# A causal 31-tap convolution on four engines: eight taps moved to TensorE by shifted copies, VectorE's chunks staggered, six z blocks last

## What is computed

```python
def _odd_mixer(h, w_in, conv_w, conv_b, ln_g, ln_b, w_out):
    proj = h @ w_in                                # 1024 -> 3 * 1024
    val, gt, z = proj[:, :1024], proj[:, 1024:2048], proj[:, 2048:]
    g = val * sigmoid(gt)
    c = depthwise_causal_conv(g, conv_w)           # 31 taps, per channel
    c = c + conv_b
    cc = c - mean(c, channels)
    var = mean(cc * cc, channels)
    c = cc * rsqrt(var + LN_EPS) * ln_g + ln_b
    y = silu(c) * silu(z)
    return y @ w_out                               # then residual, final norm
```

## Time and profile before

| | us |
|---|---|
| median of three runs | 2760.51 (2759.78 to 2760.76) |
| the profiled execution | 2754.84 |
| its span | 2753.1 |
| mean granted TensorE clock | 0.948 |

### The profile page before, as it was taken

How to read it: one execution, slowest core, us unless ns; L and a number is a source line. 1 busy time by engine, 2 the same in 40 slices (tenths; PEclk the granted TensorE clock), 3 DMA queues, 4 the chain that set the end, 5 groups by cost and what they waited for, 6 DMA issues and landing times. The chain is left out here.

```text
span 2753.1 us, 31632 instructions
## 1 busy us (share of the span) xinstructions
PE 2559.3 (93%) x11316; PEld 2065.6 (75%) x11316; DVE 989.8 (36%) x1557; ACT 992.3 (36%) x1337; POOL 1294.9 (47%) x683
## 2 busy tenths in 40 slices
PE   8999999999999999999998889999999986978777
PEld 6888878656888888888885777788888875766556
DVE  3223130164522213322113612543223169214973
ACT  5333323376433333333332323343333332224442
POOL 5555544301555544555542433246555453346843
PEclk9999999899999999999998999889999988988998
DMA  3324323201232332232331221023233322321211
GB/s 137 96 94 134 111 92 107 77 1 32 76 99 92 99 107 77 99 97 94 101 106 54 71 83 61 1 77 100 94 96 99 107 80 66 83 76 62 64 58 62
DMA packets 69332, 228.34 MB, mean 83 GB/s; under 512 B 8804, under 2 KB 13284, under 8 KB 69133
## 3 DMA queue, kind: packets, MB, share of 16 engines
q1 hardware_dynamic: 63456, 218.63, 24.9%
q10 hardware_dynamic: 4956, 5.61, 0.8%
q0 software_dynamic: 848, 3.15, 0.3%
HBM read 222.75 MB, written 6.84 MB: 83 GB/s over the span
## 5 line engine op out<-in xcount | busy, mean ns | idle before, releaser
L366 POOL TENSOR_TENSOR wl_sb<-raw_sb,wh_sb 128x1024 fp32r<-128x1024 f32 x401 | 973.2, 2430 | 1055.5 <-ACT wh_sb L358 1052.1
L1651 PE MATMUL banks<-xh_sb,wh_sb 128*128 128x512 f32 x2064 | 815.7, 395 | 72.8 <-POOL wl_sb L366 56.2
L1652 PE MATMUL banks<-xh_sb,wl_sb 128*128 128x512 f32 x2064 | 810.6, 393 | 0.0
L1653 PE MATMUL banks<-xl_sb,wh_sb 128*128 128x512 f32 x2064 | 810.2, 393 | 0.0
L358 ACT ACTIVATE wh_sb<-raw_sb 128x1024 fp32r<-128x1024 f32 x401 | 423.8, 1059 | 809.7 <-DMA raw_sb<-weights 805.5
L1651 PEld LDWEIGHTS banks<-xh_sb,wh_sb 128*128 128x128 f32 x2064 | 392.4, 190 | 163.8 <-issue 53.7
L1652 PEld LDWEIGHTS banks<-xh_sb,wl_sb 128*128 128x128 f32 x2064 | 392.9, 190 | 81.5
L1653 PEld LDWEIGHTS banks<-xl_sb,wh_sb 128*128 128x128 f32 x2064 | 391.9, 190 | 82.4
L1651 PE MATMUL banks<-hh_sb,wh_sb 128*128 128x512 f32 x704 | 273.9, 389 | 0.0
L1652 PE MATMUL banks<-hh_sb,wl_sb 128*128 128x512 f32 x704 | 273.9, 389 | 0.0
L1653 PE MATMUL banks<-hl_sb,wh_sb 128*128 128x512 f32 x704 | 273.9, 389 | 0.0
(11 more groups left out here) (359 smaller groups left out, 2689.9 us busy)
## 6 DMA issues: line engine op xcount, KB each, us to landing
raw_sb<-weights SPq DMA_DIRECT2D x404, 512.0 KB, 3.5
scratch<-scratch ACTq DMA_DIRECT2D x1, 2560.0 KB, 12.2
x_sb<-x_in SPq DMA_DIRECT2D x8, 256.0 KB, 9.2
mix_sb<-scratch POOLq DMA_DIRECT2D x1, 2048.0 KB, 8.9
out<-hf_sb SPq DMA_DIRECT2D x8, 256.0 KB, 2.1
turn<-mix_sb SPq DMA_DIRECT2D x4, 256.0 KB, 4.6
mix_sb<-turn SPq DMA_DIRECT2D x4, 256.0 KB, 4.3
turn<-mix_sb ACTq DMA_DIRECT2D x4, 256.0 KB, 2.5
```

The lines of the kernel that those rows point to most:

```text
L366: pool.tensor_tensor(wl[:, slot, :], raw[:, slot, :], wh_f[:, slot, :], ALU.subtract).then_inc(w_split, 1)
L1651: pe.matmul(dst, wh[:, q, cols], in_hi, start=first, stop=False)
L1652: pe.matmul(dst, wl[:, q, cols], in_hi, start=False, stop=False)
L1653: return pe.matmul(dst, wh[:, q, cols], in_lo, start=False, stop=last)
```

## The change

- **Taps.** TensorE gets taps 0 to 7, VectorE taps 8 to 26 (19), ScalarE with GpSimd taps 27 to 30 (4).
- **TensorE's taps.** For each chunk SP issues 16 copies inside SBUF (`shifted`): for each partition quarter q (32 channels) and each shift j = 0 to 3, 32 rows of 516 columns go to partitions 32j to 32j+31 of `moved`. A matmul then contracts over 128 partitions, which are 4 taps x 32 channels, against a 128x32 matrix of tap weights (`tap_mat`, built by GpSimd, 128x512 for two chunks), and writes 32 output partitions with a tile position of its own. Eight matmuls of 512 columns a chunk (4 quarters, 2 groups of taps), all plain float32, go to bank 6 or 7 (`conv_taps`). TensorE issues them three blocks after the chunk's g block.
- ScalarE copies that bank out and adds the bias (`keep_pe_sum`), GpSimd adds it to the other taps' sum (`add_pe_sum`), both four blocks after the g block.
- **Order of GpSimd and ScalarE.** The additions of a chunk no longer stand together behind its gate product, but one and two blocks later; products and sums have two sets of buffers.
- **Order of VectorE.** A round takes the second ten steps of chunk c-1 alternating with the first ten of chunk c, so that chunk c starts as soon as its own gate product is there; nine rounds in all, the first and the last with one chunk alone.
- **Order of blocks.** `vgvgvgvgzvgvgzvgvgzzzzzz`: two z blocks stand among the v and g blocks, six stand last. All loops over the 24 blocks are written out.
- **Order on SP.** The 16 copies of a chunk wait for its gate product and stand between the weight loads: after the load of block b for which block b-4 was a g block.

```diff
-POOL_TAPS = 7
+TAPS_PE, TAPS_DVE, TAPS_POOL = 8, 19, 4
+ROWS_TAP = 32
+for _kind in "vgvgvgvgzvgvgzvgvgzzzzzz":
+    ODD.append((_kind, _of[_kind]))
+GATE_AT = {c: b for b, (kind, c) in enumerate(ODD) if kind == "g"}
...
+        def shifted(sp, c):
+            sp.wait_ge(g_mul, c + 1)
+            if c >= 2:
+                sp.wait_ge(pe_taps, c - 1)
+            for j in range(4):
+                for q in range(4):
+                    rows, dst = slice(ROWS_TAP * q, ROWS_TAP * (q + 1)), slice(ROWS_TAP * j, ROWS_TAP * (j + 1))
+                    sp.dma_start(moved[c % 2][dst, q, :], gpad[rows, c, j:j + LONG]).then_inc(g_moved[c % 2], 16)
+
+        def odd_in_tensor(pe, first_three):
+            def conv_taps(c):
+                pe.wait_ge(g_moved[c % 2], 256 * (c // 2 + 1))
+                pe.wait_ge(tap_weights, c // 2 + 1)
+                if c >= 2:
+                    pe.wait_ge(pe_kept, c - 1)
+                for a in range(TAPS_PE // 4):
+                    for q in range(4):
+                        last = pe.matmul(banks[ROWS_TAP * q:ROWS_TAP * (q + 1), 6 + c % 2, :],
+                                         tap_mat[c // 2 % 2][:, 8 * (c % 2) + 2 * q + a, :],
+                                         moved[c % 2][:, q, 4 * a:4 * a + T], start=(a == 0), stop=(a == 1),
+                                         tile_position=(0, ROWS_TAP * q))
+                last.then_inc(pe_taps, 1)
+
+            first_three("odd.in", "odd")
+            for b in range(3, len(ODD)):
+                pe.wait_ge(w_split, BLK["odd.in"] + b + 1)
+                if b >= 4:
+                    pe.wait_ge(tiles_freed, FREE0 + TILE["odd.in"] + b - 3)
+                block_mm(pe, lin[b % 4], b % 4, xh, xl)
+                for c in range(KD):
+                    if b == GATE_AT[c] + 3:
+                        conv_taps(c)
...
+            for b, (kind, c) in enumerate(ODD):
+                if b:
+                    high_part(act, "odd.in", b % 4, b - b % 4)
+                for other in range(KD):
+                    if b == GATE_AT[other] + 1:
+                        tap_products(other)
+                    if b == GATE_AT[other] + 4:
+                        keep_pe_sum(other)
+                act.wait_ge(blocks_done, BLK["odd.in"] + b + 1)
...
+            for c in range(KD + 1):
+                for n in range(half):
+                    if c > 0:
+                        tap_step(c - 1, half + n)
+                    if c < KD:
+                        tap_step(c, n)
...
-            loads(first + 12, BLOCKS)
+            loads(first + 12, BLK["odd.in"])
+            for b in range(len(ODD)):
+                some([BLK["odd.in"] + b])
+                if b >= 4 and ODD[b - 4][0] == "g":
+                    shifted(sp, ODD[b - 4][1])
+            loads(BLK["odd.out"], BLOCKS)
...
+            for b, (kind, c) in enumerate(ODD):
+                if b:
+                    low_part(pool, "odd.in", b % 4, b - b % 4)
+                if kind == "v" and c % 2 == 0:
+                    weights_of_taps(c // 2)
+                for other in range(KD):
+                    if b == GATE_AT[other] + 1:
+                        add_tap(other, 1)
+                        add_tap(other, 2)
+                    if b == GATE_AT[other] + 2:
+                        add_tap(other, 3)
+                    if b == GATE_AT[other] + 4:
+                        add_pe_sum(other)
+                if kind == "g":
+                    gated(b, c)
```

More of the change, by code:

```diff
@@ L89 @@
                   ("ssm_d", 4), ("conv_b", 8), ("ln_g", 8), ("ln_b", 8), ("head_g", 8), ("conv_w", 31 * 8),
-                  ("mconv_w", 4 * 16), ("log_dt", 16), ("a_re", 16), ("a_im", 16), ("b_i", 1), ("b_f", 1)):
+                  ("tap_w", 64), ("mconv_w", 4 * 16), ("log_dt", 16), ("a_re", 16), ("a_im", 16), ("b_i", 1), ("b_f", 1)):
     VEC[_name] = _c
@@ L98 @@
 C_ID, C_TRI, C_ONE, C_INV = 0, P, 2 * P, 3 * P
-NCONST = C_INV + 64
+C_STACK = C_INV + 64
+NCONST = C_STACK + ROWS_TAP
+ODD, _of = [], {"v": 0, "g": 0, "z": 0}
+for _kind in "vgvgvgvgzvgvgzvgvgzzzzzz":
+    ODD.append((_kind, _of[_kind]))
+    _of[_kind] += 1
+GATE_AT = {c: b for b, (kind, c) in enumerate(ODD) if kind == "g"}
 def skewed(scratch):
@@ L238, in build @@
         tap_prod = sem("tap_prod")
-        tap_sum = sem("tap_sum")
+        tap_sum = [sem(f"tap_sum{i}") for i in range(2)]
+        o_tap = [sem(f"o_tap{i}") for i in range(2)]
+        g_moved = [sem(f"g_moved{i}") for i in range(2)]
+        tap_weights = sem("tap_weights")
+        pe_taps = sem("pe_taps")
+        pe_kept = sem("pe_kept")
         std_ready = sem("std_ready")
@@ L459, in credits_vector @@
             dve.memset(unused(), 0.0).then_inc(conv_act, 2)
-            dve.memset(unused(), 0.0).then_inc(tap_sum, 1)
         def halve_vector(dve):
@@ L1481, in build @@
         tap_acc = sig_o
-        taps = [region(17408 + T * j, T) for j in range(POOL_TAPS)]
+        taps = [[region(17408 + T * (TAPS_POOL * q + j), T) for j in range(TAPS_POOL)] for q in range(2)]
+        pe_sum = [rstd[:, :], acc[:, :]]
+        LONG = T + 4
+        moved = [buf.rearrange("p (q n) -> p q n", n=LONG) for buf in (region(21504, 4 * LONG), hf_f[:, 0:4 * LONG])]
+        tap_mat = [hf_f[:, 4 * LONG + 512 * q:4 * LONG + 512 * (q + 1)].rearrange("p (s n) -> p s n", n=ROWS_TAP)
+                   for q in range(2)]
@@ new lines, in conv_weight, with conv_bank @@
+        def conv_weight(c, tap):
+            col = VEC["conv_w"] + CONV_K * c + tap
+            return vec[:, col:col + 1]
+        def conv_bank(c):
+            return banks[:, 4 + c % 2, :]
+        def shifted(sp, c):
[6 more added lines that the diff above has]
+                    sp.dma_start(moved[c % 2][dst, q, :], gpad[rows, c, j:j + LONG]).then_inc(g_moved[c % 2], 16)
@@ L1484, in odd_tensor @@
         def odd_tensor(pe):
             for c in range(KD):
-                pe.wait_ge(o_conv, c + 3)
+                pe.wait_ge(o_conv, c + 1)
                 last = pe.matmul(banks[:, 6, :], ones, cc[:, c, :], start=(c == 0), stop=(c == KD - 1))
@@ L1493, in odd_scalar @@
             act.wait_ge(o_v, 1)
[L1494 to L1518, removed]
+            def tap_products(c):
+                act.wait_ge(g_mul, c + 1)
+                if c >= 2:
+                    act.wait_ge(tap_sum[c % 2], TAPS_POOL * (c // 2) - 1)
+                for j in range(TAPS_POOL):
+                    tap = CONV_K - TAPS_POOL + j
+                    act.activation(taps[c % 2][j], gpad[:, c, tap:tap + T], ACT.Copy,
+                                   scale=conv_weight(c, tap)).then_inc(tap_prod, 1)
@@ new lines, in keep_pe_sum @@
+            def keep_pe_sum(c):
+                act.wait_ge(pe_taps, c + 1)
+                if c >= 2:
+                    act.wait_ge(tap_sum[c % 2], TAPS_POOL * (c // 2))
+                bias = VEC["conv_b"] + c
+                act.activation(pe_sum[c % 2], banks[:, 6 + c % 2, :], ACT.Identity,
+                               bias=vec[:, bias:bias + 1]).then_inc(pe_kept, 1)
+            for b, (kind, c) in enumerate(ODD):
[8 more added lines that the diff above has]
+                if kind == "g":
+                    act.activation(gpad[:, c, PAD:PAD + T], lin[(b - 1) % 4], ACT.Copy)
+                    act.activation(sig_o[:, c, :], lin[b % 4], ACT.Sigmoid).then_inc(tiles_freed, 2)
+                if kind == "z":
+                    act.activation(zz[:, c, :], lin[b % 4], ACT.Silu).then_inc(tiles_freed, 1)
@@ L1533, in odd_vector @@
             dve.memset(gpad[:, :, 0:PAD], 0.0).then_inc(o_v, 1)
-            dve.memset(mean[:, 0:8], 0.0).then_inc(o_conv, 2)
             dve.wait_ge(o_v, 1)
[L1536 to L1556, removed]
@@ new lines, in odd_vector, with tap_step @@
+            done = [0, 0]
+            half = (TAPS_DVE + 1) // 2
+            def tap_step(c, n):
+                s, tap = c % 2, TAPS_PE + n
+                if n == TAPS_DVE:
+                    dve.wait_ge(o_tap[s], done[s])
+                    dve.wait_ge(tap_sum[s], TAPS_POOL * (c // 2 + 1))
+                    tt(cc[:, c, :], conv_bank(c), tap_acc[:, c, :], ALU.add).then_inc(o_conv, 1)
+                    return
+                g = gpad[:, c, tap:tap + T]
+                if n == 0:
+                    dve.wait_ge(g_mul, c + 1)
+                    if c >= 2:
+                        dve.wait_ge(o_conv, c - 1)
+                    ins = ts(conv_bank(c), g, conv_weight(c, tap), None, ALU.mult)
+                else:
+                    dve.wait_ge(o_tap[s], done[s])
+                    ins = stt(conv_bank(c), g, conv_weight(c, tap), conv_bank(c), ALU.mult, ALU.add)
+                ins.then_inc(o_tap[s], 1)
+                done[s] += 1
@@ L1805, in _ @@
             spread_rate(pe, EVENT["odd.pre"], diag_post, 7)
-            linear("odd.in", "odd")
+            odd_in_tensor(pe, first_three)
             odd_tensor(pe)
@@ L2119, in _ @@
```

(36 more changed lines are left out.)

## The result

| | before | after |
|---|---|---|
| median, us | 2760.15 (4 runs) | 2785.82 (2783.78 to 2787.81, 4 runs) |
| ratio | | 1.0093, 95% interval 1.0076 to 1.0111 |
| profiled execution, its span | 2754.84, 2753.1 | 2787.81, 2786.0 |

A forecast was written before the change was run, and what follows sets the result against it. VectorE and GpSimd at about 16.3 us a chunk, with TensorE's tail close behind, bound the section. Last gate product at 2638.6, section end 2667.5 instead of 2660.3 (+7.2): 2760.5 + 7.2, rounded 2768 us; range 2747 to 2786.

The forecast's parts named there:

- the loop through SP's issues, the load, the two weight parts and the gate product: From one gate product's end to the next, the weight load waiting behind SP's copies: 18.3 us, against 16.3 before.
- I take 0.47, the rate of this same queue in a row of issues: On SP's queue, each of 16 copy issues takes 0.47 us, 7.5 us a chunk; bounds 0.33 and 0.67.
- the landing of the loads: Weight load behind the copies on SP's queue: 3.4 us from load to landing.
- rival (3): On SP's queue, an issue costs 0.67 us, as on ScalarE's queue: 25 us more, 2793 us; chance 0.13.
- The sign would have turned at 0.41: On SP's queue, the end moves 127 us per us of an issue, so slower turns to faster at 0.41 us.
- The steps: Seven steps between gate products: three of 17.0, two of 18.3, two of 21.9 us, 131.4 in all, last ending at 2638.6.
- The tail: After the last gate product: chunk 7's copies land at 2648.5, taps 1.7, three blocks 16.3, clock 1, ending at 2667.5.
- The four quarters: TensorE's eight tap matmuls a chunk run at once on four column quarters, taking 1.7 us instead of 6.9.
- Rival (2): On TensorE, the quarters run one after another, 6.9 us a chunk: 17 us slower, 2777 us; chance 0.20.
- What was charged at nothing: Copies' traffic in the section, and TensorE's waits for copies before chunks 0 to 6, up to 2.7 us each: no cost.
- VectorE's waits: VectorE idles 4 to 5 us a round, waiting for the gate product or for GpSimd's sum.
- rival (1): On SP's queue, issues are cheap at 0.33 us: 10.6 us faster, 2750 us; chance 0.25, shared with SP never deciding.

The follow-up runs named there:

- run 1: Changed kernel with each chunk's 16 copies placed behind one weight load more on SP: 2739.8 us, ratio 0.9945 to the kernel before.
- run 2: Changed kernel with the same bytes in 4 copies of 128 rows a chunk instead of 16, taps' data wrong: 2729.0 us, ratio 0.9900 to the kernel before.
- run 4: Changed kernel with 8 copies a chunk instead of 16 (shifts 2 and 3 left out, taps wrong): 2741.4 us, ratio 0.9945 to the kernel before.
- run 7: Changed kernel with 8 of each chunk's 16 copies issued by ScalarE, the other 8 by SP: 2743.6 us, ratio 0.9964 to the kernel before.
- run 3: Changed kernel with 16 copies a chunk, each moving 129 of 516 columns, taps wrong: 2787.4 us, ratio 1.0112 to the kernel before.
- run 5: Changed kernel with the 16 copies written to DRAM instead of SBUF, taps on stale data: 2765.5 us, ratio 1.0044 to the kernel before.
- run 8: Changed kernel with copies split over SP and ScalarE and, on SP, behind one weight load more: 2728.2 us, ratio 0.9904 to the kernel before.
- run 6: Changed kernel's order only, no taps on TensorE and no copies, taps split 24 to 7: 2737.8 us, ratio 0.9942 to the kernel before.

## Why the prediction was right where it was, and where it fell short

**The mechanism** was the forecast one: the loop through SP's issues, the load, the two weight parts and the gate product. The step from 2508.68 to 2529.24 shows it link by link, and runs 1, 2, 4 and 7 by moving or removing issues on SP; in run 3 the issues stay and so does the time.

**The term that was mis-sized** is "I take 0.47, the rate of this same queue in a row of issues". All of the earlier trace rows have DRAM at one end., the only rows with SBUF at both ends, said 0.65 to 0.71, and I took them for a matter of ScalarE's queue; they were the nearest rows in kind. Measured: 0.63 apart. By the prediction's own slope of 127 us for each us of an issue, 0.16 more is 20.3 us, and 7.2 + 20.3 = 27.5; measured in the section 31.4. The remaining 3.9 are mostly the landing of the loads, below. That the medians differ by only 25.7, close to 27.5, is the spread between executions and no confirmation. The way (slower) and the mechanism were right, the size was far too small (7.2 against 31.4), and that the result still lies in the range, by 0.2 us, is luck: rival (3), 0.67 an issue and 2793, came within 7 us of it. The sign would have turned at 0.41, and the median issue inside SBUF was 0.59 or more in every run.

**The steps.** Forecast 131.4 us for seven, measured 152.5 (2508.68 to 2661.18); 7 x 2.5 (16 issues in 10.0 instead of 7.5) is 17.5 of the difference. A load behind the copies lands after 3.9 us (2519.32 to 2523.21) instead of 3.4, which is about another 3.5. The copies' traffic is not the reason, since it is 3.9 in run 3 as well; the 3.4 came from a lone load, and here a second load is issued directly behind the first, which was not tried apart. In run 5, with issues as assumed, the seven steps sum to 134.8. (Among the readings of the kernel before, GpSimd's terms for a chunk add up to 16.5 and not 16.2; its gate products stand 16.1 apart on average, and nothing in the forecast rests on the difference.)

**The tail.** Forecast 28.9 us, measured 32.0. The issues of chunk 7 took 2.6 us more and their landing 0.7 less. The taps took 3.64 instead of 1.7, behind a wait of 5.43 us where 2 were forecast, at a granted clock of 0.50. The blocks behind them took 16.6, 0.7 less than the forecast with its 1 us for the clock. In run 5 the tail is 28.9.

```profile
2672.93 3.64 PE L1525 MATMUL banks<-hf_sb 128*32 128x512 f32 x16 [5.43 <-DMA hf_sb<-mix_sb]
```

**The four quarters** run at once: eight tap matmuls take 3.2 to 3.6 us in the changed kernel, where TensorE has waited for them and its granted clock is 0.50 to 0.58, and 1.92 in run 8 at 1.00, where one after another they would need 6.88. The forecast of 1.7 holds only for the second case. Rival (2) is out.

**What was charged at nothing.** The copies' traffic costs nothing that can be seen (run 3). The waits of TensorE for the copies of chunks 0 to 6 (3.9 to 7.4 us each, where up to 2.7 were forecast) were hidden in the changed kernel, as stated. In a shorter loop they need not be; run 8 has none after chunk 0's.

**VectorE's waits** were forecast at 4 to 5 us a round. It is idle for 7.6 us of a step of 21.0 and for 11.1 of one of 24.5 (a z block in between), since the loop is longer.

**The page's rule** on the time to initiate a DMA, "usually small relative to the DMA itself" (the Trainium skill, "DMA: Bandwidth & Descriptors", "Issuing engines are not separate DMA queues"), is no guide to the time of this pattern. A single issue is shorter than its DMA here too: 0.59 us, against 2.0 from issue to landing in the median. But 16 issues in a row take 10 us, with four times fewer bytes as well, and a load waits behind them. The estimate of 4.4 us in rival (1) used the same page's fit of 2.0 us plus bytes over 436 GB/s, which it gives for a DMA issued by GpSimd, as if the 16 copies of SP were one such DMA, which is not this case. The measurement decides.

**Where the expected gain went.** By ratio to the kernel before: reordering alone 0.9942, with copies and taps 1.0093, with copies in a better place and on two queues 0.9904. So the taps on TensorE are worth about 0.4% beyond the reordering once their copies are well placed (9.6 us by the medians of runs 6 and 8, 5.8 by the spans of their profiled executions; the slowest execution of run 8 is faster than the fastest of run 6). In the changed kernel the place of the copies and their single queue cost 1.9%, more than the reordering and the taps bring together.

## What to carry to other kernels

Before putting DMAs on a queue that also feeds a pipeline, add their issue times and ask which load stands behind them and who waits for it; a loop such as load, split, gate, copy is found by following the program order of each queue, and not by the busy shares. Put the load first, use fewer and larger copies where the layout allows, and split long rows of issues over two queues. Price an issue from a row with the same ends (SBUF to SBUF, SBUF to DRAM), even when that row is of another engine.

## What the runs showed of the hardware

- An issue of a copy with SBUF at both ends takes, in the median, 0.59 us on SP with 32 rows of 516 or 129 columns and 0.60 with 128 rows of 516 (runs 2 and 3), and 0.61 to 0.62 on ScalarE (32 rows of 516, run 7). One from SBUF to DRAM takes 0.43 on SP (run 5). Why was not tried.
- Float32 matmuls on the four column quarters of TensorE, each over 128 partitions, run at once: eight of 512 columns take 1.92 us at a granted clock of 1.00 (run 8) and 3.64 at 0.50 (changed kernel, chunk 7).
- SP and ScalarE issued copies at the same time, and SP's eight took 5.0 to 5.4 us beside ScalarE's eight (run 7) as without them (run 4), but for one chunk.
- ScalarE's queue issued copies while its tap products ran: the first issue at 2506.79, the first product from 2506.78 to 2507.50 (run 7).
